# Down products with 64 slots and 512 weight columns at a time, and output rows moved 64 at a time, in a hybrid decoder block with 32 experts

## The chip, the cores and the metric

One Trainium2 chip, one core. The time is the device time of one launch in microseconds (us); the runs before the change took 1283.56 to 1284.55 us, with a median of 1284.49 us over 3 runs.

## The reference

A decoder block of 512 tokens and 1024 features: a gated linear recurrence and a dilated attention share one input and one output projection; a mixture of experts follows. The change touches only the latter. Cut to it (`h` are 512 normed rows, each token goes to 4 of 32 experts):

```python
logits = (h @ router_w + router_b).astype(jnp.float32)
top_vals, top_idx = lax.top_k(logits, TOP_K)
gates = jax.nn.softmax(top_vals, axis=-1)
...
def expert_block(args):
    xb, e = args
    u = xb @ w_up[e] + b_up[e]
    return _clamped_swiglu(u) @ w_down[e] + b_down[e]
...
y = ybuf[dest] * gates.reshape(-1)[order][:, None].astype(ybuf.dtype)
return jnp.zeros((N, D), h.dtype).at[sorted_tok].add(y)
```

All is float32. `w_up` is 1024 x 2048 and `w_down` 1024 x 1024 per expert, 12 MB together, so 384 MB of weights are read once. A final RMS norm over each row ends the block.

## The kernel before, in words

The kernel is written engine by engine: each engine has its own function with a fixed order of instructions and waits on semaphores. The first 300 us are projections, recurrence, attention and routing. Then come 32 steps, one per expert, in an order of experts by their load.

**Slots.** An expert takes its tokens in groups of 32 slots (`STEP`). Experts at place 0, 1 and the odd places to 29 have `BIG` = 3 groups (96 slots), the 16 others `LESS` = 2 (64 slots); `groups(p)` says which. Tokens beyond that go through further blocks at the end (`nx`), of which this input has none in its profile.

**TensorE's step** (`moe_step`, line 2174) for place p: bias rows of the up product (`up_bias`, L2072), 8 chunks of the up product (`up_chunk`, L2081), and, behind chunks 2 and 5, one turn each of the *move* of the outputs of expert p-2 (`move_turn`, L2153). Then the down product of expert p-1 (`down_chunk`, L2098), 4 chunks of two halves.

In up and down products the slots are the stationary operand, 32 columns wide, and the weights stream. Four such products stand beside each other in the array, one for each quarter of the output columns: `quarter(j)` chooses 32 output partitions. So the 32 rows of a group lie in four quarters of the partitions, each with 256 of the 1024 output features:

```python
ins = pe.matmul(Yp2[quarter(j), g, :], As[:, g, 2 * c + h, :], raw[q.slot(m)][:, at_w:at_w + 256],
```

**Outputs.** ACT scales the down product by the gates and writes its high part (fp32r) to SBUF (`y_highs`, L898), DVE the rest as low part (`y_lows`, L1571), per group. DVE makes for each group a 0/1 matrix that says which token a slot holds (`token_sels`, L1578). The move multiplies that matrix (stationary, 32 rows x 128 tokens) with high and low part, adding up in PSUM over groups and parts for each of 4 token tiles (`i`); DVE then adds PSUM to the rows `X` (`add_tile`, L1584). Before a down product TensorE waits for the low parts of the expert before (`y_low`) and, with 96 slots, for the adds.

**Weights.** SP loads pairs of chunks (2 MB) into 9 buffers; each load waits until TensorE has used the buffer (`chunk_used`), L562.

**Tail.** The last two experts' outputs go half by half of the features: `pair_chunk` (L2117), `last_chunk` (L2129), `move_half` (L2140). `move_half` takes two phases, with a wait between them, since two row groups may not write one bank at the same time. ACT's and DVE's `add_half` (L1591), squares, root and scaling end the program.

## Time and profile before

| | us |
|---|---|
| median of 3 runs (lowest, highest) | 1284.49 (1283.56, 1284.55) |
| the profiled execution, its own time | 1284.0 |
| its span, first to last instruction | 1282.2 |
| TensorE busy | 1245.9 (97%) |
| VectorE busy | 554.7 (43%) |
| ScalarE busy | 238.6 (19%) |
| GpSimd busy | 122.7 (10%) |

The profile is of one execution. The expert steps begin at about 300 us and end at 1266 us. In the rows, PE is TensorE's matmuls, PEld its weight loads, DVE VectorE, ACT ScalarE, POOL GpSimd, SP the engine that issues the DMAs. A matmul of fp32 stands in the trace as two records (192 for the 96 matmuls of a down product with 96 slots). Starts of matmuls are recorded; their ends are modelled. The granted TensorE clock is 1.00 of full speed in all stretches used below.

### The profile page before, as it was taken

How to read it: one execution, taken by the hardware profiler on the slowest of the kernel's cores; microseconds unless marked ns; L12 is line 12 of the kernel's file. 1: busy time of each engine (PE TensorE's matmuls, PEld its weight loads, DVE VectorE, ACT ScalarE, POOL GpSimd, SP SyncE). 2: the span in 40 equal slices, each digit the busy share in tenths (PEclk: the TensorE clock that was granted, in tenths of full speed). 3: DMA queues.
4: the chain of work that ended last, by engine and by line, in shares of the span. 5: the costliest groups of instructions: out<-in, count | busy, mean ns of one | idle time of the engine just before them, and what ended most of it. 6: DMA issues, size and time to landing. Idle time of an engine off the chain costs nothing.

```text
span 1282.2 us, 33934 instructions
## 1 busy us (share of the span) xinstructions
PE 1245.9 (97%) x15007; PEld 680.1 (53%) x15008; DVE 554.7 (43%) x1066; ACT 238.6 (19%) x463; POOL 122.7 (10%) x127
## 2 busy tenths in 40 slices
PE   6999999999999999999999999999999999999994
PEld 5888887884455544444444444444444454444442
DVE  5657648665544533333333424233323333332423
ACT  6354436421100001000000001000100000000104
POOL 0000005200110110101010101010110101010001
PEclk9999999999999999999999999999999999999998
DMA  8422208069899999999999999999999999999983
GB/s 241 134 66 82 84 1 331 21 264 423 346 412 380 416 426 419 425 424 423 423 423 424 423 425 423 424 422 425 421 423 423 423 424 424 423 423 424 424 353 144
DMA packets 69547, 444.26 MB, mean 346 GB/s; under 512 B 6537, under 2 KB 35821, under 8 KB 44721
## 3 DMA queue, kind: packets, MB, share of 16 engines
q1 hardware_dynamic: 65696, 433.61, 82.6%
q0 software_dynamic: 3696, 8.38, 1.8%
q8 instruction: 123, 2.02, 0.6%
q14 instruction: 32, 0.25, 0.1%
HBM read 439.10 MB, written 4.72 MB: 346 GB/s over the span
## 4 chain that ended last, share of the span: by engine, by line
PE 92%; DMA 4%; DVE 2%; ACT 1%; issue 1%; SPq 0%; DVEq 0%
PE psum L2081 43%; PE psum L2098 20%; PE psum L1807 9%; PE psum L2153 6%; PE psum L1804 3%; DMA w_raw_pair<-w_down 3%; PE psum L2072 2%; PE psum L1892 2%; PE psum L1950 1%; PE psum L1925 1%; PE psum L2129 1%; PE psum L1967 1%; DMA shape_consts<-shape_constants 1%; PE psum L1769 1%; PE psum L1905 1%
## 5 line engine op out<-in xcount | busy, mean ns | idle before, releaser
L2081 PE MATMUL psum<-w_raw_pair,x_slots_turned 128*32 128x512 f32 x4928 | 551.0, 594 | 2.0 <-DVE x_slots_turned L1649 0.7
L2081 PEld LDWEIGHTS psum<-w_raw_pair,x_slots_turned 128*32 128x32 f32 x4928 | 168.5, 110 | 317.7 <-issue 296.9
L1584 DVE TENSOR_TENSOR x_rows<-x_rows,psum 128x1024 f32<-128x1024 f32 x120 | 141.1, 1217 | 330.7 <-PE psum L2153 330.7
L2098 PE MATMUL psum<-w_raw_pair,a_slots 128*32 128x256 f32 x4864 | 272.3, 379 | 1.2 <-DMA w_raw_pair<-w_down 1.1
L2098 PEld LDWEIGHTS psum<-w_raw_pair,a_slots 128*32 128x32 f32 x4864 | 164.9, 110 | 116.0 <-issue 21.8
L889 ACT ACTIVATE lin<-psum 128x768 f32<-128x768 f32 (+1 forms) x32 | 22.5, 704 | 606.3 <-PE psum L2081 606.3
L1553 DVE STREAM_TRANSPOSE a_slots<-glu 128x768 f32<-128x768 f32 (+1 forms) x31 | 26.3, 849 | 183.4 <-PE psum L2098 183.4
L2153 PEld LDWEIGHTS psum<-y_part_group,token_sel 32*128 32x128 f32 x2432 | 76.7, 184 | 48.7 <-issue 48.6
L686 POOL COPY gather_quarters<-row_quarters 128x2 int32 (+1 forms) x30 | 16.5, 550 | 761.1 <-DVE x_slots_turned L1548 704.3
L2153 PE MATMUL psum<-y_part_group,token_sel 32*128 32x256 f32 x2432 | 88.8, 287 | 0.0
L898 ACT ACTIVATE y_part_group<-psum,gate_t 128x256 fp32r<-128x256 f32 x76 | 31.0, 471 | 255.6 <-PE psum L2098 245.0
L691 POOL DMA_INDIRECT gathered_quarters<-normed_rows,gather_quarters x74 | 74.7, 1010 | 39.3 <-POOL gather_quarters L686 24.7
L1807 PE MATMUL psum<-h_low,w_in_high 128*128 128x512 f32 x160 | 63.3, 396 | 0.0
L1807 PE MATMUL psum<-h_high,w_in_high 128*128 128x512 f32 x160 | 62.3, 389 | 0.0
L1807 PE MATMUL psum<-h_high,w_in_low 128*128 128x512 f32 x160 | 62.3, 389 | 0.0
L1548 DVE STREAM_TRANSPOSE x_slots_turned<-gathered_quarters 128x256 f32<-128x256 f32 x74 | 43.5, 631 | 42.2 <-PE psum L2081 40.4
L1571 DVE SCALAR_TENSOR_TENSOR y_part_group<-psum,gate_t,y_part_group 128x256 fp32r<-128x256 f32 x76 | 32.6, 478 | 22.9 <-ACT y_part_group L898 22.9
L1070 DVE TENSOR_TENSOR w_in_low<-w_in_raw,w_in_high 128x1024 fp32r<-128x1024 f32 x24 | 29.0, 1221 | 17.2 <-ACT w_in_high L768 17.2
L1807 PEld LDWEIGHTS psum<-h_low,w_in_high 128*128 128x128 f32 x160 | 30.1, 188 | 6.9 <-issue 0.6
L1807 PEld LDWEIGHTS psum<-h_high,w_in_low 128*128 128x128 f32 x160 | 30.0, 188 | 6.4
L1807 PEld LDWEIGHTS psum<-h_high,w_in_high 128*128 128x128 f32 x160 | 30.1, 188 | 5.8
L1578 DVE TENSOR_SCALAR token_sel<-token_numbers,slot_tokens 128x512 fp32r<-128x512 f32 x76 | 32.6, 480 | 0.0
(312 smaller groups left out, 990.8 us busy)
## 6 DMA issues: line engine op xcount, KB each, us to landing
w_raw_pair<-w_up SPq DMA_DIRECT2D x128, 2048.0 KB, 26.5
w_raw_pair<-w_down SPq DMA_DIRECT2D x60, 2048.0 KB, 25.5
w_in_raw<-w_in SPq DMA_DIRECT2D x28, 512.0 KB, 3.8
w_raw_pair<-w_down SPq DMA_DIRECT2D x8, 1024.0 KB, 36.6
w_buf<-w_out SPq DMA_DIRECT2D x4, 1024.0 KB, 11.1
x_rows<-x SPq DMA_DIRECT2D x4, 512.0 KB, 5.3
x_rows<-x SPq DMA_DIRECT2D x1, 2048.0 KB, 13.2
normed_rows<-h_rows SPq DMA_DIRECT2D x4, 512.0 KB, 4.5
```

The lines of the kernel that those rows point to most:

```text
L691: pool.indirect_dma_start(XQ[:, g, :], None, normed_dram.rearrange("r (j f) -> (r j) f", j=4), bass.IndirectOffsetOnAxis(IDXQ[:, g:g + 1], 0),
L898: ins = act.activation(YP[0][g][:, :], banks[:, g, :], ACT.Copy, scale=gate_t[:, g, bass.ds(column, 1)])
L1070: ins = dve.tensor_tensor(WPL[:, c % 4, :, :], WPR[:, c % 2, :, :], WPH[:, c % 4, :, :].bitcast(F32), ALU.subtract)
L1548: ins = dve.transpose(xq[:, g, :, :], XQ[:, g, :].rearrange("p (i k) -> p k i", k=DK))
L1571: ins = dve.scalar_tensor_tensor(YP[1][g][:, :], banks[:, g, :], gate_t[:, g, bass.ds(column, 1)], YP[0][g][:, :].bitcast(F32), ALU.mult, ...
L1578: ins = dve.tensor_scalar(sels[g][:, :], tokens[:, :], slot_tok[:, g, bass.ds(column, 1)], None, ALU.is_equal)
L1584: dve.tensor_tensor(x_tile, x_tile, PS[:, first_bank:first_bank + 4, half], ALU.add).then_inc(added, 1)
L1804: ins = pe.matmul(blocks_of(o), h_part[:, k, j * P:(j + 1) * P], w_rows, start=(k == 0 and h_part is HL), stop=(k == DK - 1 and w_part is ...
L1807: ins = pe.matmul(o, w_part[:, j, k, :], h_part[:, k, :], start=(k == 0 and h_part is HL), stop=(k == DK - 1 and w_part is WPL))
L2081: ins = pe.matmul(U[quarter(j), g, :], slots, up_columns(w, j), start=False, stop=(c == UPC - 1))
L2098: ins = pe.matmul(Yp2[quarter(j), g, :], As[:, g, 2 * c + h, :], raw[q.slot(m)][:, at_w:at_w + 256], start=(c + h == 0 and g % 2 == 0), st ...
L2153: ins = pe.matmul(PS[:, MOVE_BANK + j, i % 2 * 256:i % 2 * 256 + 256], SELT[g][quarter(j), i * P:(i + 1) * P], YP[part][g][quarter(j), :], ...
```

## The change

The three groups no longer stand alike. The first two become one *wide* group of 64 slots, the third stays as it is.

- Down product: the wide group is a stationary operand of 64 columns, two pieces beside each other (`side(j)`: 64 partitions), each against 512 weight columns. With 96 slots the third group follows in the same half chunk, 4 pieces of 32 columns against 256.
- `a_slots` is laid out so that 64 or 96 slots are adjacent; DVE's transpose writes it with another stride.
- ACT and DVE write high and low part of the wide group with one instruction of 512 columns (`Y_wide`), and of the third with one of 256. Token matrices are 2 for 96 slots, 1 for 64.
- Moves: the wide group is moved in pieces of 64 rows. With 64 slots, 2 matmuls of 512 columns per tile and part. With 96 slots, 4 of 256 columns, then the third group's 4 of 32 rows, for each tile and each part.
- Tail: the same with 256 columns; the phases and their waits fall away, and DVE may add the first two tiles when `half_moved` is signalled. The copies to `slot_pair` and `gate_pair` go.

```diff
--- before.py
+++ after.py
+PAIR = LESS * STEP
+WIDE, THIRD = range(2)
+GROUP_IN = ((0, 1, 0, 1), (2, 2, 2, 2))
...
-        As = over("a_slots", [P, BIG, 2 * DNC, STEP], xg0 + 13312)
-        As_last = over("a_slots_last", [P, LESS, 2 * DNC, STEP], xg0 + 4096)
+        As = over("a_slots", [P, 2 * DNC, BLK], xg0 + 13312)
+        As_last = over("a_slots_last", [P, 2 * DNC, PAIR], xg0 + 4096)
...
-        y_piece_at = [[oa0, oa0 + 1024, oa0 + 4096], [oa0 + 2048, oa0 + 3072, oa0 + 5120]]
-        YP = [[over(f"y_part{part}_group{g}", [P, 256], y_piece_at[part][g], F32R) for g in range(BIG)] for part in range(2)]
-        YP_last = [[YP[part][2], over(f"y_last_part{part}", [P, 256], xg0 + 2048 + part * 1024, F32R)] for part in range(2)]
+        YW = [over(f"y_wide_part{part}", [P, HALF], oa0 + part * 2048, F32R) for part in range(2)]
+        YT = [over(f"y_third_part{part}", [P, 256], oa0 + 4096 + part * 1024, F32R) for part in range(2)]
+        YP = [[over(f"y_part{part}_half{n}", [P, 256], oa0 + part * 2048 + n * 1024, F32R) for n in range(2)] for part in range(2)]
+        YP_last = [[YT[part], over(f"y_last_part{part}", [P, 256], xg0 + 2048 + part * 1024, F32R)] for part in range(2)]
...
+        Y_wide, Y_third = PS[:, 3, :], Yp2[:, LESS, :]
...
+        def side(j):
+            return slice(j * PAIR, (j + 1) * PAIR)
...
-            def y_highs(n, column, banks):
-
-                for g in range(n):
-                    ins = act.activation(YP[0][g][:, :], banks[:, g, :], ACT.Copy, scale=gate_t[:, g, bass.ds(column, 1)])
-                    if g:
-                        ins.then_inc(y_high, 1)
+            def y_highs(n, column):
+
+                act.activation(YW[0][:, :], Y_wide, ACT.Copy, scale=gate_t[:, WIDE, bass.ds(column, 1)]).then_inc(y_high, 1)
+                if n == BIG:
+                    act.activation(YT[0][:, :], Y_third, ACT.Copy, scale=gate_t[:, THIRD, bass.ds(column, 1)]).then_inc(y_high, 1)
...
             def a_rows(q, n, slots):
                 dve.wait_ge(a_ready, q + 1)
-                dve.transpose(slots[:, 0:n, :, :].rearrange("p g b s -> p (g b s)"), GL[:, 0:n, :].rearrange("p g f -> p (g f)")
-                              ).then_inc(a_turned, 1)
+                dve.transpose(slots[:, :, 0:n * STEP].rearrange("p b (g s) -> p g b s", s=STEP),
+                              GL[:, 0:n, :].rearrange("p g (b f) -> p g b f", f=STEP)).then_inc(a_turned, 1)
...
-            def y_lows(highs, n, column, banks):
-
-                for g in range(n):
-                    if g != 1:
-                        dve.wait_ge(y_high, highs + max(g, 1))
-                    ins = dve.scalar_tensor_tensor(YP[1][g][:, :], banks[:, g, :], gate_t[:, g, bass.ds(column, 1)],
-                                                   YP[0][g][:, :].bitcast(F32), ALU.mult, ALU.subtract)
+            def y_lows(highs, n, column):
+
+                dve.wait_ge(y_high, highs + 1)
+                ins = dve.scalar_tensor_tensor(YW[1][:, :], Y_wide, gate_t[:, WIDE, bass.ds(column, 1)], YW[0][:, :].bitcast(F32),
+                                               ALU.mult, ALU.subtract)
+                if n == BIG:
+                    dve.wait_ge(y_high, highs + 2)
+                    ins = dve.scalar_tensor_tensor(YT[1][:, :], Y_third, gate_t[:, THIRD, bass.ds(column, 1)], YT[0][:, :].bitcast(F32),
+                                                   ALU.mult, ALU.subtract)
                 ins.then_inc(y_low, 1)
 
-            def token_sels(n, column, sels):
-
-                for g in range(n):
-                    ins = dve.tensor_scalar(sels[g][:, :], tokens[:, :], slot_tok[:, g, bass.ds(column, 1)], None, ALU.is_equal)
+            def token_sels(n, column):
+
+                ins = dve.tensor_scalar(SELT[0][:, :], tokens[:, :], slot_tok[:, WIDE, bass.ds(column, 1)], None, ALU.is_equal)
+                if n == BIG:
+                    ins = dve.tensor_scalar(SELT[1][:, :], tokens[:, :], slot_tok[:, THIRD, bass.ds(column, 1)], None, ALU.is_equal)
                 ins.then_inc(token_sel, 1)
...
+            def add_tile(i, n):
+
+                if n == BIG:
+                    x_tile = X[:, i, :].rearrange("p (j f) -> p j f", j=4)
+                    sums = PS[:, MOVE_BANK:MOVE_BANK + 4, i % 2 * 256:i % 2 * 256 + 256]
+                else:
+                    x_tile = X[:, i, :].rearrange("p (j f) -> p j f", j=2)
+                    sums = PS[:, MOVE_BANK + 2 * (i % 2):MOVE_BANK + 2 * (i % 2) + 2, :]
+                dve.tensor_tensor(x_tile, x_tile, sums, ALU.add).then_inc(added, 1)
...
             def add_half(n, i):
 
+                if i < 2:
+                    dve.wait_ge(S("half_moved"), n + 1)
+                else:
+                    dve.wait_ge(moved, NE * 2 - 2 + 2 * n)
...
-            def pair_columns():
-
-                for g in range(2):
-                    r = slice(2 * g * STEP, 2 * (g + 1) * STEP)
-                    dve.tensor_copy(slot_pair[r, :], slot_tok[r, g, 0:NE])
-                    ins = dve.tensor_copy(gate_pair[r, :], gate_t[r, g, 0:NE])
-                ins.then_inc(S("pair_columns"), 1)
...
             def down_chunk(q, m, c, n):
                 if c % 2 == 0:
                     pe.wait_ge(raw_landed[q.slot(m) // 2], q.landed(m))
+                w = raw[q.slot(m)]
                 for h in range(2):
-                    for g in range(n):
+                    first, last = c + h == 0, c == DNC - 1 and h == 1
+                    for j in range(2):
+                        at_w = h * D + j * HALF
+                        ins = pe.matmul(Y_wide[side(j), :], As[:, 2 * c + h, 0:PAIR], w[:, at_w:at_w + HALF], start=first, stop=last)
+                    if n == BIG:
                         for j in range(4):
                             at_w = h * D + j * 256
-                            ins = pe.matmul(Yp2[quarter(j), g, :], As[:, g, 2 * c + h, :], raw[q.slot(m)][:, at_w:at_w + 256],
-                                            start=(c + h == 0 and g % 2 == 0), stop=(c == DNC - 1 and h == 1),
-                                            skip_group_check=True)
+                            ins = pe.matmul(Y_third[quarter(j), :], As[:, 2 * c + h, PAIR:BLK], w[:, at_w:at_w + 256],
+                                            start=first, stop=last)
                 ins.then_inc(chunk_used, 1)
...
+            def move_half(n, tiles, sel, parts, first):
+
+                for i in tiles:
+                    for part in range(2):
                         for j in range(2):
+                            ins = pe.matmul(PS[:, HALF_BANKS[n][i // 2][j], i % 2 * 256:i % 2 * 256 + 256], sel[side(j), i * P:(i + 1) * P],
+                                            parts[part][side(j), :], start=(first and i % 2 + part == 0), stop=(not first and part == 1),
+                                            skip_group_check=True)
+                    if not first and i == 1:
+                        ins.then_inc(S("half_moved"), 1)
...
             def move_turn(turn, n, first):
 
                 pe.sem_inc(S("moves_begun"), 1)
                 for i in (2 * turn, 2 * turn + 1):
-                    for g in range(n):
-                        for part in range(2):
+                    tile, cols = slice(i * P, (i + 1) * P), slice(i % 2 * 256, i % 2 * 256 + 256)
+                    for part in range(2):
+                        if n == BIG:
+                            for w in range(2):
+                                for j in range(2):
+                                    pe.matmul(PS[:, MOVE_BANK + 2 * j + w, cols], SELT[0][side(j), tile], YW[part][side(j), w * 256:w * 256 + 256],
+                                              start=(first and i % 2 + part == 0), stop=False, skip_group_check=True)
                             for j in range(4):
-                                ins = pe.matmul(PS[:, MOVE_BANK + j, i % 2 * 256:i % 2 * 256 + 256], SELT[g][quarter(j), i * P:(i + 1) * P],
-                                                YP[part][g][quarter(j), :], start=(first and i % 2 + g + part == 0),
-                                                stop=(g == n - 1 and part == 1), skip_group_check=True)
+                                ins = pe.matmul(PS[:, MOVE_BANK + j, cols], SELT[1][quarter(j), tile], YT[part][quarter(j), :],
+                                                start=False, stop=(part == 1), skip_group_check=True)
+                        else:
+                            for j in range(2):
+                                ins = pe.matmul(PS[:, MOVE_BANK + 2 * (i % 2) + j, :], SELT[0][side(j), tile], YW[part][side(j), :],
+                                                start=(part == 0), stop=(part == 1))
                 ins.then_inc(moved, 1)
...
-            move_half(0, 0, SELT[0], (YP[0][0], YP[1][0]), True).then_inc(S("crossed"), 1)
+            move_half(0, (0, 1), SELT[0], (YP[0][0], YP[1][0]), True)
             last_chunk(0, 1)
-            pe.wait_ge(S("crossed"), 1)
-            move_half(0, 1, SELT[0], (YP[0][0], YP[1][0]), True).then_inc(moved, 1)
+            move_half(0, (2, 3), SELT[0], (YP[0][0], YP[1][0]), True).then_inc(moved, 1)
             last_chunk(1, 0)
             pe.wait_ge(token_sel, NE)
             pe.wait_ge(S("first_low"), 1)
-            pe.wait_ge(moved, NE * 2 - 3)
-            move_half(0, 0, SELT_last, (YP_last[0][0], YP_last[1][0]), False).then_inc(S("crossed"), 1)
-            pe.wait_ge(S("crossed"), 2)
-            move_half(0, 1, SELT_last, (YP_last[0][0], YP_last[1][0]), False).then_inc(moved, 1)
+            move_half(0, range(TT), SELT_last, (YP_last[0][0], YP_last[1][0]), False).then_inc(moved, 1)
             last_chunk(1, 1)
             pe.wait_ge(added, ADDS - 2 * TT + 2)
-            move_half(1, 0, SELT[0], (YP[0][1], YP[1][1]), True).then_inc(S("crossed"), 1)
-            pe.wait_ge(S("crossed"), 3)
-            move_half(1, 1, SELT[0], (YP[0][1], YP[1][1]), True).then_inc(moved, 1)
+            move_half(1, range(TT), SELT[0], (YP[0][1], YP[1][1]), True).then_inc(moved, 1)
             pe.wait_ge(y_low, NE)
-            pe.wait_ge(moved, NE * 2 - 1)
-            move_half(1, 0, SELT_last, (YP_last[0][1], YP_last[1][1]), False).then_inc(S("crossed"), 1)
-            pe.wait_ge(S("crossed"), 4)
-            move_half(1, 1, SELT_last, (YP_last[0][1], YP_last[1][1]), False).then_inc(moved, 1)
+            move_half(1, range(TT), SELT_last, (YP_last[0][1], YP_last[1][1]), False).then_inc(moved, 1)
```

On TensorE, the down product of a 96-slot expert, with the end of the up product before it and the bias and up product behind it. Columns: line, operation, output and inputs, size of the output, count. `w_raw_pair_123` and `_115` hold two chunks each; before:

```order
L2081 MATMUL psum<-w_raw_pair_122,x_slots_turned 32x512 x16
L2098 MATMUL psum<-w_raw_pair_123,a_slots 32x256 x48
L2098 MATMUL psum<-w_raw_pair_115,a_slots 32x256 x48
L2072 MATMUL psum<-bias_up_parts,bias_sel_up 32x512 x12
L2081 MATMUL psum<-w_raw_pair_116,x_slots_turned 32x512 x24
```

The same place with the change:

```order
L2094 MATMUL psum<-w_raw_pair_122,x_slots_turned 32x512 x16
L2112 MATMUL psum<-w_raw_pair_123,a_slots 64x512 x2
L2116 MATMUL psum<-w_raw_pair_123,a_slots 32x256 x4
...
L2112 MATMUL psum<-w_raw_pair_115,a_slots 64x512 x2
L2116 MATMUL psum<-w_raw_pair_115,a_slots 32x256 x4
...
L2085 MATMUL psum<-bias_up_parts,bias_sel_up 32x512 x12
L2094 MATMUL psum<-w_raw_pair_116,x_slots_turned 32x512 x24
```

The 96 matmuls of one size became 16 of 64 columns and 32 of 32 columns, which alternate 8 times.

On TensorE, one turn of a move of 96 slots, between two chunks of the up product (`y_part_group` and `token_sel` are the parts and token matrices of a group); before:

```order
L2081 MATMUL psum<-w_raw_pair_117,x_slots_turned 32x512 x12
L2153 MATMUL psum<-y_part_group_134,token_sel_161 128x256 x4
L2153 MATMUL psum<-y_part_group_137,token_sel_161 128x256 x4
L2153 MATMUL psum<-y_part_group_135,token_sel_162 128x256 x4
L2153 MATMUL psum<-y_part_group_138,token_sel_162 128x256 x4
L2153 MATMUL psum<-y_part_group_136,token_sel_163 128x256 x4
L2153 MATMUL psum<-y_part_group_139,token_sel_163 128x256 x4
...
L2081 MATMUL psum<-w_raw_pair_117,x_slots_turned 32x512 x12
```

With the change:

```order
L2094 MATMUL psum<-w_raw_pair_117,x_slots_turned 32x512 x12
L2169 MATMUL psum<-y_wide_part_134,token_sel_161 128x256 x4
L2172 MATMUL psum<-y_third_part_136,token_sel_162 128x256 x4
L2169 MATMUL psum<-y_wide_part_135,token_sel_161 128x256 x4
L2172 MATMUL psum<-y_third_part_137,token_sel_162 128x256 x4
...
L2094 MATMUL psum<-w_raw_pair_117,x_slots_turned 32x512 x12
```

The rows stand for one of the two tiles of a turn. 12 groups of four matmuls with 32 rows became 8: in turn four matmuls with 64 rows (L2169) and four with 32 (L2172).

## Rows read from the trace of the kernel before

**Rows 1.** Busy time of each engine in a stretch, with granted clock and DMA.

```profile
core 0: us, PE busy (x) PEld busy (x) DVE busy (x) ACT busy (x) POOL busy (x), PEclk, DMA share, GB/s
500.00:1200.00 700.00, 697.58 (x9646) 315.40 (x9642) 239.36 (x339) 59.16 (x129) 73.28 (x83) 1.00 1.01 423
```

**Rows 2.** DMA issues (us to landing) from 340 to 400, then from 1100 to 1200.

```profile
w_raw_pair<-w_up SPq DMA_DIRECT2D x8, 2048.0 KB, 10.7
...
w_raw_pair<-w_up SPq DMA_DIRECT2D x14, 2048.0 KB, 37.6
```

**Rows 3.** Timeline of PE: start, us, instructions; two steps from 737 us.

```profile
737.03 10.54 PE L2098 MATMUL psum<-w_raw_pair,a_slots 128*32 128x256 f32 x192
...
755.88 1.70 PE L2153 MATMUL psum<-y_part_group,token_sel 32*128 32x256 f32 x48
757.51 7.93 PE L2081 MATMUL psum<-w_raw_pair,x_slots_turned 128*32 128x512 f32 x72
765.37 1.70 PE L2153 MATMUL psum<-y_part_group,token_sel 32*128 32x256 f32 x48
...
772.18 7.27 PE L2098 MATMUL psum<-w_raw_pair,a_slots 128*32 128x256 f32 x128
779.09 1.09 PE L2072 MATMUL psum<-bias_up_parts,bias_sel_up 96*32 96x512 bf16 x8
...
785.62 1.22 PE L2153 MATMUL psum<-y_part_group,token_sel 32*128 32x256 f32 x32
786.77 5.36 PE L2081 MATMUL psum<-w_raw_pair,x_slots_turned 128*32 128x512 f32 x48
...
796.67 3.64 PE L2098 MATMUL psum<-w_raw_pair,a_slots 128*32 128x256 f32 x64
```

**Rows 4.** Timeline of PE, then of DVE, from 1215 us to the tail.

```profile
1215.19 10.57 PE L2098 MATMUL psum<-w_raw_pair,a_slots 128*32 128x256 f32 x192 [1.10 <-DMA w_raw_pair<-w_down]
...
1252.80 1.93 PE L2129 MATMUL psum<-w_raw_pair,a_slots_last 128*32 128x256 f32 x32 [0.74 <-DMA w_raw_pair<-w_down]
1254.66 0.74 PE L2140 MATMUL psum<-y_part_group,token_sel 32*128 32x256 f32 x16
1255.34 1.93 PE L2129 MATMUL psum<-w_raw_pair,a_slots_last 128*32 128x256 f32 x32
1257.20 0.74 PE L2140 MATMUL psum<-y_part_group,token_sel 32*128 32x256 f32 x16
...
1259.92 1.56 PE L2140 MATMUL psum<-y_part_group,token_sel_last 32*128 32x256 f32 x32
1261.41 1.93 PE L2129 MATMUL psum<-w_raw_pair,a_slots_last 128*32 128x256 f32 x32
...
1264.33 1.27 DVE L1591 TENSOR_TENSOR x_rows<-x_rows,psum 128x512 f32<-128x512 f32 x2
1266.61 2.48 DVE L1591 TENSOR_TENSOR x_rows<-x_rows,psum 128x512 f32<-128x512 f32 x4 [1.01 <-PE psum L2140]
```

**Rows 5.** Timeline of PE and PEld where one product follows another.

```profile
174.08 1.12 PE L1820 MATMUL psum<-ak_T,aq_T 64*128 64x512 f32 x4
175.13 0.19 PEld L1804 LDWEIGHTS psum<-w_in_high,h_low 128*128 128x128 f32 x1 [0.76 <-issue]
...
289.08 0.41 PEld L1967 LDWEIGHTS psum<-router_w_sb,h_T 128*128 128x128 f32 x3 [0.41 <-issue]
...
747.17 0.55 PEld L2072 LDWEIGHTS psum<-bias_up_parts,bias_sel_up 96*32 96x32 bf16 x12
...
754.48 1.47 PE L2081 MATMUL psum<-w_raw_pair,x_slots_turned 128*32 128x512 f32 x12
755.88 0.19 PEld L2153 LDWEIGHTS psum<-y_part_group,token_sel 32*128 32x128 f32 x4 [0.84 <-issue]
```

**Rows 6.** Groups of instructions by line: busy, mean ns, idle before and releaser.

```profile
L1553 DVE STREAM_TRANSPOSE a_slots<-glu 128x768 f32<-128x768 f32 x16 | 15.6, 978 | 76.6 <-PE psum L2098 76.6
L898 ACT ACTIVATE y_part_group<-psum,gate_t 128x256 fp32r<-128x256 f32 x76 | 31.0, 471 | 255.6 <-PE psum L2098 245.0
```

97 lines of the change are left out of this document (41 added, 56 removed).

## The prediction

> **What bounds the kernel now.** I read the page first: TensorE is busy for 97% of the span, which proves little with pipelined matmuls. Then the stages. From 500 to 1200 us TensorE hardly stops (697.6 of 700 us), and the DMA engines are full too, at 423 GB/s [rows 1]. Which of the two sets the pace is told by the time from the issue of a weight load to its landing: 10.7 us around 370 us, 37.6 us around 1150 us [rows 2]. A load is issued when TensorE frees its buffer, so the queue grows all the time: TensorE frees buffers slightly faster than the DMAs fill them, and lives on what was loaded ahead. Its period for two experts is 796.67 - 737.03 = 59.6 us [rows 3]; the DMAs' must be a little longer. The stock lasts until about 1214 us. Only then does TensorE wait for weights, three times for long: idle for 1.10 us before 1215.19 and 0.74 before 1252.80 are the first and last [rows 4]. The ends of matmuls are modelled and lie late, 1.93 us for 8 rounds that take 1.73 (below), so some 0.2 us comes to each: 1.3, 1.3 and 0.9, together 3.5 us. So both paths end almost together. TensorE time taken out of the loop brings next to nothing, since the DMAs stay full; TensorE time put into it is paid in full beyond those 3.5 us. DVE (239 of 700 us) and ACT (59) have ample room [rows 1].
>
> **How TensorE spends a step.** The trace records each fp32 matmul as two. Four of 32 columns run side by side: 72 records of the up product are 18 rounds of four and last 7.93 us, 48 are 12 rounds and last 5.36 [rows 3]. The difference makes 0.428 us a round. From start to start the 18 rounds take 765.37 - 757.51 = 7.86 us [rows 3], 0.15 us more than their rounds, once per visit. The down product with 64 slots is 32 rounds with 256 columns in 779.09 - 772.18 = 6.91 us, 0.216 a round [rows 3], so 48 rounds with 96 slots are 10.4. A last down chunk, 8 rounds, takes 1257.20 - 1255.34 = 1.86 us [rows 4], 0.13 more than its rounds. The moves, weights of 128 columns and 32 rows: 12 rounds in 757.51 - 755.88 = 1.63 us, 8 in 786.77 - 785.62 = 1.15, 4 in 1255.34 - 1254.66 = 0.68 [rows 3, 4]. That is 0.119 us a round and 0.20 us per visit.
>
> What is this price per visit? Between down product, bias and up product, all with 32 weight columns, it does not occur: the bias's weight loads start at 747.17, while the down product's last round still streams [rows 5] (48 rounds from 737.03 end at 747.4). At a move it does. The last up round of 12 records starts at 754.48 + 2 x 0.43 = 755.34 and streams to 755.77; the move's loads start at 755.88, after 0.84 us of idle loader, against 0.30 between rounds [rows 5]. Nothing is loaded ahead: the array empties first (0.11 us), then the load itself is bare. The same is seen where only the columns change, from 32 to 128 (0.41 us idle before 289.08, behind L2001), and where only the rows do, from 64 to 128 (0.76 us before 175.13) [rows 5]. **So each change of the shape of the piece of the array in use costs 0.13 to 0.20 us**, the more the more columns are then loaded. No row has a change between 64 and 32 columns, or 64 and 32 rows. The Trainium skill, TensorEngine Tiling (Array Packing), Key Properties and Available Configurations, speaks against this change there: changing the tiling mode, as opposed to the tile, drains the engine, and 128x64 and 128x32, like 64x128 and 32x128, are listed as modes of their own.
>
> **The change, part by part.** Experts 0 and the odd ones to 29 hold 96 slots (16 experts); 14 others of the loop hold 64.
>
> *Down product, 64 slots.* 32 rounds of four (6.91 us) become 16 rounds of two with 512 columns. A round streams twice as long as before, like the up product's: 16 x 0.428 = 6.85 us. New are the entry with 64 columns and the way back to 32 for the bias. For 64 columns I take 0.16 us a visit, between 0.14 (32 columns) and 0.20 (128 columns), nearer the former. In all 6.85 + 0.16 + 0.14 - 6.91 = +0.24 us. The skill's page TensorE: Matmul & The Clock Gate, LDWEIGHTS, counts a load as columns divided by 1.2 ns, 53 ns for 64 columns against 27 for 32; by that, an estimate, the visit would be 0.17 us and the sum less than 1 us higher. No row has a load of 64 columns.
>
> *Down product, 96 slots.* Here each of the 8 halves of chunks now goes from 64 columns to 32 and back. Wide part: 0.16 + 2 x 0.428 = 1.02 us. Third: 0.14 + 2 x 0.216 = 0.57 us. 8 x 1.59 = 12.7 us instead of 10.4: **+2.3 us**. The bias behind it has 32 columns again and costs no further visit.
>
> *Moves, 64 slots.* A turn of 8 rounds at 256 columns (1.15 us) becomes 4 rounds of two with 512 columns, in one mode: 0.20 + 4 x 0.216 = 1.06; two turns, -0.18 us.
>
> *Moves, 96 slots.* A turn of 12 rounds in one visit (1.63 us) becomes four times a wide part (2 rounds, 0.20 + 0.24 = 0.44) and a third (1 round, 0.20 + 0.12 = 0.32): 4 x 0.76 = 3.03 us. **+1.40 us** a turn, +2.80 per expert.
>
> *ACT and DVE.* Of three evictions per expert at 471 ns on ACT, and their like on DVE, two become one of 512 columns: between 471 and 2 x 471 ns, so no more work in all [rows 6]. One token selection goes per expert. The transpose moves the same elements with another write stride; its price for that is not in the trace, but between nothing and twice its 978 ns it stays hidden, as DVE works a third of the time [rows 1, 6]. All of it lies beside TensorE: the low parts must be ready at the first move, 755.88 - 747.4 = 8.5 us behind the down product [rows 3], and the waits before the adds stand where they stood. If that cover were gone it would be at most 1 us an expert. Counted 0. The four pair-column copies go too, 0 as well. SP issues the same loads in the same order.
>
> *Tail.* The first two pieces keep their 4 rounds. A half moved for all four tiles was two phases with a wait between, 1261.41 - 1259.92 = 1.49 us, and is now 0.20 + 8 x 0.119 = 1.15: -0.34 us for the one ahead of the last chunk. Behind the last chunk DVE finished the first half at 1264.33 + 1.27 = 1265.60 and waited until 1266.61 [rows 4]; moves now end sooner and the first two tiles are signalled early, so it goes on at once: -1.0 us. DVE's adds are late next. Together -1.4 us.
>
> **Sum.** 16 x (2.3 + 2.8) = 81.6; 14 x (0.24 - 0.18) = 0.8; waits for weights gone, -3.5, since TensorE's period of 59.6 + 5.2 = 64.8 us is now well above what the DMAs need; tail -1.4. That is +77.5 us on the profiled execution's 1284.0: **1361.5, rounded 1362**. The median of the runs, 1284.49, is 0.5 higher, which I leave in the rounding. Bounds: 128 wide visits at 0.14 or 0.20 instead of 0.16 give -2.6 or +5.1 us. For 96 slots there are 16 x 16 = 256 visits more in the down products and 16 x 2 x 7 = 224 more in the moves; if a visit of a single round hides a third of its price, some 25 us go.
>
> **Rivals.**
>
> 1. *The array does not empty between 64 and 32.* The hardware could treat the pieces as the same small squares and load ahead, as between bias and up product. For: those two differ in rows (96 and 128) at no price [rows 5]. Against: every other change of shape in the trace pays. The rounds' streaming is the same with wide and narrow pieces, so the loop is where it was and only the tail's 1.4 us come: 1282.6, not slower. It decides when a further visit costs under 0.016 us: 480 of them then stay within the 3.5 us of waits, the tail's 1.4 and the 2.6 us that a measurement can tell. Chance 9%, a third of it faster by over 0.2%.
>
> 2. *Only changes of rows cost, columns are free.* Then the down products add nothing and the moves 16 x 2.8 = 45: 1284.0 + 45 - 3.5 - 1.4 = 1324. 5%.
>
> 3. *Two pieces of 64 columns do not run side by side.* Then every down product streams 6.85 us longer: 30 x 6.85 = 206 more, about 1567. Against: 64-row pieces do run in pairs, four records of 512 columns from 174.08 to the next load at 175.13, where one by one they would need 4 x 0.43 = 1.7 us [rows 5]. 2%.
>
> 4. *The copies are what counts:* wider evictions or the transpose hold up the next move. This would show as TensorE waiting for DVE; 8.5 us of room speak against it, at most 1 us an expert, 32 more: 1394. 2%.
>
> **How the numbers follow.** The forecast, each change of shape paid as measured, has 82%. The range 1322 to 1380 takes in rival 2, the part hidden in short visits, and upwards the 5 us for wide loads and some 13 us for visits dearer than the long ones; outside lie rivals 1, 3 and 4 and the forecast's edges, about 2 in 10. A measurement of this kernel tells 0.2% (2.6 us) from no change. Faster 3% and same 7%, rival 1 with a remainder for what I don't see; slower 90%.
>
> **What would show it.** Right: in the order of time the down product of a 96-slot expert takes 12.7 us instead of 10.4 and a move turn 3.0 instead of 1.6, with gaps before each switch between the wide and the third lines; two experts take 64.8 us; loads land about 10 us or less after their issue to the end, and no wait for weights is left. The down product of a 64-slot expert stays near 7.0 us. Wrong: if weights of the third part are loaded while the wide part streams (rival 1), if only the moves grow (2), or if the 64-slot down product takes near 14 us (3).

## The result and the profile after

The changed kernel takes **1347.87 us** (median of 4 runs, 1347.31 to 1348.94) against 1284.52 (4 runs, 1283.56 to 1285.37): a ratio of 1.0496, 95% interval 1.0484 to 1.0509, 63.4 us slower. The forecast was +77.5 us, so its sign and most of its size came, and about 14 us did not. The profiled executions, 1347.94 and 1284.0 us, differ by 63.9; the ledger below is made for these two.

Two experts, from the timeline of PE of the changed kernel (start, us, instructions), in the order of [rows 3]:

```profile
765.83 1.08 PE L2112 MATMUL psum<-w_raw_pair,a_slots 128*64 128x512 f32 x4
766.84 0.64 PE L2116 MATMUL psum<-w_raw_pair,a_slots 128*32 128x256 f32 x8
767.41 1.08 PE L2112 MATMUL psum<-w_raw_pair,a_slots 128*64 128x512 f32 x4
...
778.34 0.83 PE L2085 MATMUL psum<-bias_up_parts,bias_sel_up 96*32 96x512 bf16 x12
...
786.83 0.51 PE L2169 MATMUL psum<-y_wide_part,token_sel 64*128 64x256 f32 x4
787.27 0.39 PE L2172 MATMUL psum<-y_third_part,token_sel 32*128 32x256 f32 x4
...
789.85 7.93 PE L2094 MATMUL psum<-w_raw_pair,x_slots_turned 128*32 128x512 f32 x72
...
800.72 5.36 PE L2094 MATMUL psum<-w_raw_pair,x_slots_turned 128*32 128x512 f32 x48
806.01 7.09 PE L2112 MATMUL psum<-w_raw_pair,a_slots 128*64 128x512 f32 x32
813.03 0.61 PE L2085 MATMUL psum<-bias_up_parts,bias_sel_up 96*32 96x512 bf16 x8
813.47 5.33 PE L2094 MATMUL psum<-w_raw_pair,x_slots_turned 128*32 128x512 f32 x48
818.73 1.20 PE L2176 MATMUL psum<-y_wide_part,token_sel 64*128 64x512 f32 x8
819.85 5.36 PE L2094 MATMUL psum<-w_raw_pair,x_slots_turned 128*32 128x512 f32 x48
...
829.84 1.08 PE L2112 MATMUL psum<-w_raw_pair,a_slots 128*64 128x512 f32 x4
```

Read it from start to start. The period is 829.84 - 765.83 = 64.0 us (before 59.6, forecast 64.8). The down product of the 96-slot expert takes 778.34 - 765.83 = 12.51 us: a wide visit 1.01, a third 0.57, eight times. A move turn of a 96-slot expert takes 789.85 - 786.83 = 3.02 us, and the down product of a 64-slot expert 7.02 ("near 7.0" in the forecast). These three are within 0.2 us of the forecast; the period is 0.8 us short of it, because the 59.6 us of before held 0.8 us that was not work, as the runs below show.

The same timeline with the loader (PEld), at the first switch:

```profile
765.83 0.20 PEld L2112 LDWEIGHTS psum<-w_raw_pair,a_slots 128*64 128x64 f32 x4 [0.84 <-issue]
...
766.84 0.16 PEld L2116 LDWEIGHTS psum<-w_raw_pair,a_slots 128*32 128x32 f32 x8 [0.81 <-issue]
```

The loader stands idle for 0.81 us of the wide visit, although what it loads next has long been in SBUF: here the 32-column piece is loaded only when the wide part has streamed. The run without a change of width, below, tests whether the width is the reason. Under rival 1 this pause would have been absent.

In the stage from 500 to 1200 us (first row, columns as in [rows 1]) TensorE has no pause that the profile shows, and the DMAs now have some slack. The second row, from the DMA issues between 1100 and 1200 us, ends with the time from issue to landing of the loads of `w_up`: 12.4 us, where it was 37.6 in [rows 2]. The six loads of `w_down` took 9.3 us. The forecast said about 10 or less.

```profile
500.00:1200.00 700.00, 700.00 (x5996) 225.60 (x5992) 214.03 (x275) 52.13 (x99) 68.33 (x77) 1.00 0.98 403
```

```profile
w_raw_pair<-w_up SPq DMA_DIRECT2D x12, 2048.0 KB, 12.4
```

No wait for weights of the experts is left. The tail answers to [rows 4]. First the start of its first product in the kernel before, then PE and DVE of the changed kernel:

```profile
1243.67 5.36 PE L2117 MATMUL psum<-w_raw_pair,a_slots 128*32 128x256 f32 x96
```

```profile
1310.98 7.13 PE L2133 MATMUL psum<-w_raw_pair,a_slots 128*64 128x256 f32 x64
...
1325.29 1.21 PE L2153 MATMUL psum<-y_third_part,token_sel_last 64*128 64x256 f32 x16
1326.43 1.95 PE L2144 MATMUL psum<-w_raw_pair,a_slots_last 128*64 128x256 f32 x16
```

```profile
1329.34 3.67 DVE L1614 TENSOR_TENSOR x_rows<-x_rows,psum 128x512 f32<-128x512 f32 x6
```

A half for all four tiles is moved in 1326.43 - 1325.29 = 1.14 us (1.49 before), and DVE adds six times without a pause, where it had stood for 1.01 us.

### The profile page after: what moved, and what is told of

It reads as the page before. It is cut to its first block, busy times and chain, and to the rows that moved or that the text cites. A ratio compares the mean times of both kernels' runs of the same rounds, so it can differ in the third digit from the quotient of the medians.

```text
span 1346.1 us, 25227 instructions
## 1 busy us (share of the span) xinstructions
PE 1315.6 (98%) x10751; PEld 577.3 (43%) x10752; DVE 536.3 (40%) x994; ACT 231.2 (17%) x431; POOL 123.0 (9%) x127
## 3 DMA queue, kind: packets, MB, share of 16 engines
q8 instruction: 91, 1.49, 0.5%
## 4 chain that ended last, share of the span: by engine, by line
PE 95%; DVE 2%; ACT 1%; issue 0%; DMA 0%; SPq 0%; DVEq 0%; ACTq 0%
PE psum L2094 41%; PE psum L2112 17%; PE psum L1820 8%; PE psum L2116 5%; PE psum L2169 4%; PE psum L1817 3%; PE psum L2172 3%; PE psum L2176 2%; PE psum L1905 1%; PE psum L2085 1%; PE psum L1963 1%; PE psum L1938 1%; PE psum L1980 1%; PE psum L2144 1%; PE psum L2133 1%; PE psum L1918 1%
## 5 line engine op out<-in xcount | busy, mean ns | idle before, releaser
L2094 PEld LDWEIGHTS psum<-w_raw_pair,x_slots_turned 128*32 128x32 f32 x4928 | 151.7, 110 | 335.5 <-issue 324.2
L2112 PE MATMUL psum<-w_raw_pair,a_slots 128*64 128x512 f32 x960 | 237.3, 607 | 0.0
L2112 PEld LDWEIGHTS psum<-w_raw_pair,a_slots 128*64 128x64 f32 x960 | 56.2, 135 | 127.2 <-issue 127.2
L2116 PE MATMUL psum<-w_raw_pair,a_slots 128*32 128x256 f32 x1024 | 81.8, 391 | 0.0
L903 ACT ACTIVATE y_wide_part<-psum,gate_t 128x512 fp32r<-128x512 f32 x30 | 20.6, 687 | 274.7 <-PE psum L2116 179.8
L2116 PEld LDWEIGHTS psum<-w_raw_pair,a_slots 128*32 128x32 f32 x1024 | 20.1, 108 | 103.9 <-issue 103.9
L2169 PE MATMUL psum<-y_wide_part,token_sel 64*128 64x256 f32 x512 | 64.4, 330 | 0.0
L2169 PEld LDWEIGHTS psum<-y_wide_part,token_sel 64*128 64x128 f32 x512 | 38.1, 184 | 38.2 <-issue 25.8
L2172 PE MATMUL psum<-y_third_part,token_sel 32*128 32x256 f32 x512 | 50.0, 379 | 0.0
L2176 PE MATMUL psum<-y_wide_part,token_sel 64*128 64x512 f32 x224 | 33.5, 417 | 0.0
```

The costliest lines, as they stand in the source:

```text
L2094: ins = pe.matmul(U[quarter(j), g, :], slots, up_columns(w, j), start=False, stop=(c == UPC - 1))
L2112: ins = pe.matmul(Y_wide[side(j), :], As[:, 2 * c + h, 0:PAIR], w[:, at_w:at_w + HALF], start=first, stop=last)
L2116: ins = pe.matmul(Y_third[quarter(j), :], As[:, 2 * c + h, PAIR:BLK], w[:, at_w:at_w + 256], start=first, stop=last)
L2169: pe.matmul(PS[:, MOVE_BANK + 2 * j + w, cols], SELT[0][side(j), tile], YW[part][side(j), w * 256:w * 256 + 256], start=(first and i % 2 + ...
L2172: ins = pe.matmul(PS[:, MOVE_BANK + j, cols], SELT[1][quarter(j), tile], YT[part][quarter(j), :], start=False, stop=(part == 1), skip_grou ...
L2176: ins = pe.matmul(PS[:, MOVE_BANK + 2 * (i % 2) + j, :], SELT[0][side(j), tile], YW[part][side(j), :], start=(part == 0), stop=(part == 1))
```

## The experiments

Weights, instructions and data stay as in the changed kernel unless a text says otherwise. The visits come first, then the 14 us that the forecast had too much.

### One move turn, two visits instead of eight

```diff
-                for i in (2 * turn, 2 * turn + 1):
+                for wide in ((True, False) if n == BIG else (True,)):
+                    for i in (2 * turn, 2 * turn + 1):
...
-                        if n == BIG:
+                            if n == BIG and wide:
...
+                            elif n == BIG:
```

> The changed kernel, with the output move of a 96-slot expert written in another order: in each turn first the 64-slot parts of both tiles and both parts, then the thirds, so that TensorE changes its array piece 2 times a turn and not 8. The same instructions otherwise. Theory (the price is paid at each change of piece, 0.20 us for a visit of the 64-column piece and one of the 32-column piece together with the exposed load): a turn of 3.02 us has 8 visits of about 0.17 us, 6 of them go, so a turn takes about 1.9 to 2.0 us; 2 turns times 16 experts, so 34 to 38 us less, 1310 to 1314 us. Rival (the thirds and the 64-slot parts are slow for another reason, the instructions of the two column halves or writes to the same bank, whatever their order): a turn stays at 3.0 us and the time at 1348 us.

Measured: 1310.74 us (4 runs, 1310.17 to 1312.09; ratio to the kernel before 1.0208, 1.0193 to 1.0224), 37.1 us under the changed kernel. Its timeline of PE has one turn as

```profile
770.74 1.22 PE L2170 MATMUL psum<-y_wide_part,token_sel 64*128 64x256 f32 x16
771.88 0.74 PE L2174 MATMUL psum<-y_third_part,token_sel 32*128 32x256 f32 x16
772.55 0.64 PE L2094 MATMUL psum<-w_raw_pair,x_slots_turned 128*32 128x512 f32 x4
```

772.55 - 770.74 = 1.81 us for the same 32 records that took 3.02. Six visits fewer save 1.2 us: 0.20 each, the price of the prediction. The expectation had 0.17 a visit, and so a turn of 1.9 to 2.0 us: a turn gained slightly more than that. The rival (3.0 us whatever the order) falls.

### The down product in four visits instead of sixteen

```diff
+            def down_pair(q, m, c):
...
+                for wide in (True, False):
+                    for k in range(2):
+                        w = raw[q.slot(m + k)]
+                        for h in range(2):
...
+                            for j in range(2 if wide else 4):
```

> The changed kernel, with the down product of a 96-slot expert written in another order: for each pair of weight chunks first the 64-slot products of its four halves, then the thirds, so that there are 4 visits of pieces an expert and not 16. The same instructions otherwise. Theory (each visit costs 0.14 to 0.16 us over its streaming): 12 visits less, 1.7 to 1.9 us of the 12.5 us that the down product takes, 16 experts: 27 to 31 us less, 1317 to 1321 us. Rival (only the second sort of products is slow, or the two sorts hide each other's loads as they stand): 12.5 us stay, 1348 us.

Measured: 1320.53 us (4 runs, 1320.10 to 1321.01; ratio 1.0283, 1.0267 to 1.0299), 27.3 us less. From its timeline of PE:

```profile
754.07 3.65 PE L2132 MATMUL psum<-w_raw_pair,a_slots 128*64 128x512 f32 x16
757.65 1.93 PE L2135 MATMUL psum<-w_raw_pair,a_slots 128*32 128x256 f32 x32
759.52 3.65 PE L2132 MATMUL psum<-w_raw_pair,a_slots 128*64 128x512 f32 x16
763.10 1.93 PE L2135 MATMUL psum<-w_raw_pair,a_slots 128*32 128x256 f32 x32
764.85 0.40 PE L2085 MATMUL psum<-bias_up_parts,bias_sel_up 96*32 96x512 bf16 x4
```

10.78 us instead of 12.51: 1.73 / 12 = 0.144 us a visit.

### Both orders

> The changed kernel with both orders at once: per 96-slot expert 12 visits less in the down product and 12 less in the moves. Theory: the two gains add, 61 to 69 us, which gives 1279 to 1287 us; an expert pair would take about 60 us, and by then the weights' loads are as late as in the kernel before, so the waits for them come back and the end is bounded near 1281 to 1285 us. Rival (the gains are not of the array but of what lies beside it): less than the sum, 1300 us or more.

Measured: 1282.38 us (11 runs, 1281.64 to 1284.26; ratio 0.9987, 0.9978 to 0.9996). Both savings add: 1347.9 - 37.1 - 27.3 = 1283.5. One term of the expectation was wrong in kind. DMA stands at 424 GB/s again in the window from 500 to 1200 us, but TensorE's 700.00 us of that window show no wait for weights:

```profile
500.00:1200.00 700.00, 700.00 (x6426) 246.06 (x6426) 224.47 (x289) 55.01 (x104) 73.45 (x83) 1.00 1.01 424
```

So 12 + 12 visits less per 96-slot expert are worth the whole loss in time: **order alone turns 5% slower into no slower**. The visits that stay still cost: a down product of 10.78 + 0.11 us against 10.36 and a turn of 1.81 against 1.63 make some 14 us over 16 experts. They are offset by about as much lost time that the kernel before has and this one has not, which is the subject of the last sections.

### No change of width, the same alternation

```diff
-                            ins = pe.matmul(Y_third[quarter(j), :], As[:, 2 * c + h, PAIR:BLK], w[:, at_w:at_w + 256],
-                                            start=first, stop=last)
+                            ins = pe.matmul(Y_third[side(j % 2), :], As[:, 2 * c + h, STEP:BLK], w[:, at_w:at_w + 256],
+                                            start=first, stop=last, skip_group_check=True)
```

> The changed kernel, where the third group's down products of a 96-slot expert hold 64 slots too (the last 64 of the 96) in 64-column pieces, four matmuls of 256 weight columns for a half of a chunk; both column halves are added in one place, so the third group's products are not those of the reference. The two sorts of products alternate as before, but no piece changes width. Theory (the change of the piece's width drains the array): a half of a chunk is 0.86 us for the first group and 0.86 us for the third, the down product takes about 13.8 us and no load stands bare after a product; 16 experts, about 1368 us. Rival (it is the alternating of groups, stationary data or target that costs, whatever the width): the pauses stay, about 2.0 us a half and 16.3 us a product, about 1408 us.

Measured: 1372.95 us (one run; the kernel before had a median of 1282.26 on that chip). From its timelines of PE and PEld:

```profile
777.23 1.08 PE L2112 MATMUL psum<-w_raw_pair,a_slots 128*64 128x512 f32 x4
778.14 1.03 PE L2116 MATMUL psum<-w_raw_pair,a_slots 128*64 128x256 f32 x8
779.01 1.03 PE L2112 MATMUL psum<-w_raw_pair,a_slots 128*64 128x512 f32 x4
779.87 0.39 PE L2116 MATMUL psum<-w_raw_pair,a_slots 128*64 128x256 f32 x2
```

```profile
777.72 0.14 PEld L2116 LDWEIGHTS psum<-w_raw_pair,a_slots 128*64 128x64 f32 x2 [0.28 <-issue]
```

Here the third's weights are loaded at 777.72, while the wide part still streams until about 778.1 (0.28 us of idle loader, not 0.81). After the first visit a half of a chunk takes 0.87 + 0.86 us, all streaming, and the whole product 13.9 (its bias starts at 791.16). The theory had 1368 us, the rival 1408. So in the down product groups, targets and data alternate at no price that these rows show; it is the piece's width that costs. For the moves the kernel before is the like case: its turn alternates three groups and two parts, all with 32 rows, in one visit of 1.63 us.

### The new layout without the mixed experts

```diff
-                    for j in range(2):
+                    for j in range(2 if n == LESS else 0):
...
-                    if n == BIG:
+                    for g in range(BIG if n == BIG else 0):
...
-                            ins = pe.matmul(Y_third[quarter(j), :], As[:, 2 * c + h, PAIR:BLK], w[:, at_w:at_w + 256],
+                            ins = pe.matmul(Yp2[quarter(j), g, :], As[:, 2 * c + h, quarter(g)], w[:, at_w:at_w + 256],
```

> The changed layout for 64-slot experts and the tail only; 96-slot experts as in the kernel before (three groups of 32 slots, no 64-column piece). Theory: the loss sits entirely in the 96-slot experts, so it goes: 1280 to 1284 us, against 1284.5 before; the bias block of a 64-slot step takes 0.44 us and not 1.21 to 1.25 us, the tail is about 1.2 us shorter, and the rest of the gain is taken by waits for weights, since loads bound the kernel then. Rival (the 64-slot experts have a cost of their own in the new layout, which the 96-slot ones hide): above 1286 us.

Measured: 1278.48 us (5 runs, 1278.07 to 1280.64; ratio **0.9959**, 0.9945 to 0.9972): faster than both kernels, by 5.8 us (0.4%) against the one before. Timeline of PE at a 64-slot step, then its two largest waits for weights (us in total, times, longest; with two smaller ones 7.7 us). The profile is of the slowest of the five, 1280.64 us:

```profile
767.27 7.09 PE L2121 MATMUL psum<-w_raw_pair,a_slots 128*64 128x512 f32 x32
774.29 0.61 PE L2094 MATMUL psum<-bias_up_parts,bias_sel_up 96*32 96x512 bf16 x8
774.73 0.60 PE L2103 MATMUL psum<-w_raw_pair,x_slots_turned 128*32 128x512 f32 x4
```

```profile
PE psum L2125 <- DMA w_raw_pair<-w_down: 4.4, 4, 1.3
PE psum L2142 <- DMA w_raw_pair<-w_down: 1.7, 2, 1.1
```

The bias block behind the 64-slot down product takes 0.44 us. In the kernel before it takes 779.09 to 780.30 = **1.21 us** [rows 3 has its start]; here is the row behind it:

```profile
780.30 1.96 PE L2081 MATMUL psum<-w_raw_pair,x_slots_turned 128*32 128x512 f32 x16
```

Two rounds of 0.216 us need 0.44. Nothing that the profile names is waited for. At two places the loader's next load starts only 0.66 and 0.69 us after the one before it (idle for 0.57 and 0.60 us in its timeline), among instructions that wait for nothing late: the pair of weights that comes next landed 15 us earlier, and the semaphores that stand before the bias and the first up round were raised 5 us earlier. This is the term that the forecast did not have. The next runs ask what it is.

### The 64-slot down product in as many instructions as before

In the changed kernel, then in the kernel just above, a half of a chunk takes 8 matmuls of 128 weight columns and not 2 of 512 (the edit in the changed kernel):

```diff
+                    for k in range(1 if n == BIG else 4):
+                        cols = HALF if n == BIG else P
...
-                        at_w = h * D + j * HALF
+                            at_w = h * D + j * HALF + k * cols
+                            ins = pe.matmul(Y_wide[side(j), k * cols:(k + 1) * cols], As[:, 2 * c + h, 0:PAIR], w[:, at_w:at_w + cols],
+                                            start=(first and k == 0), stop=last, skip_group_check=True)
```

> The changed kernel, with the down product of a 64-slot expert cut into pieces of 128 weight columns: the same columns stream through the same pieces of the array, but by four times as many matmuls and loads. Theory (the 1.21 to 1.25 us of the bias block ahead of each 64-slot step in the kernel before is TensorE waiting for its next instructions, after a product of many short ones): the bias block of a 64-slot step goes from 0.44 us back to about 1.2 us or more, the product itself takes 7.0 us or little more; 14 steps, so 10 us or more on top: 1358 us or more. Rival (that time in the kernel before has to do with the 32-column pieces): 0.44 us stay and the time is 1348 us.

Measured: 1349.94 us (4 runs, 1349.41 to 1350.57; ratio 1.0527, 1.0507 to 1.0548), and 0.44 us for each of the bias blocks: by the words of the expectation the rival. One of them, behind a down product that started at 807.21 (7.14 us):

```profile
814.35 0.61 PE L2085 MATMUL psum<-bias_up_parts,bias_sel_up 96*32 96x512 bf16 x8
814.79 0.60 PE L2094 MATMUL psum<-w_raw_pair,x_slots_turned 128*32 128x512 f32 x4
```

But the run was on a chip where the kernel before takes 1282.26 us (7 runs, 1279.50 to 1284.52) and not 1284.3, which matters below.

> The kernel with the changed layout for 64-slot experts and the tail only, with the down product of a 64-slot expert cut into pieces of 128 weight columns: as many matmuls and loads as in the kernel before at the same place, with the moves of the 96-slot experts ahead of them as dense as there, but in 64-column pieces. Theory (TensorE takes its instructions faster than they are supplied through dense moves followed by a dense down product, and runs dry at the bias block behind them): the bias block of a 64-slot step takes 1.2 us again and not 0.44 us; the waits for weights shrink by part of it, so 1279 to 1284 us. Rival (the 0.8 us belong to the 32-column pieces of the 64-slot down product): 0.44 us stay and the time is that of the kernel without the cut, 1278 to 1279 us.

Measured: 1284.34 us (11 runs, 1282.24 to 1286.16; ratio 0.9998, 0.9989 to 1.0007), 5.9 us more than without the cut. This is yet another chip; the kernel before takes 1284.24 on it, and 1284.26 on that of the run without the cut. Timeline of PE:

```profile
774.38 7.20 PE L2122 MATMUL psum<-w_raw_pair,a_slots 128*64 128x128 f32 x126
781.76 0.38 PE L2122 MATMUL psum<-w_raw_pair,a_slots 128*64 128x128 f32 x2 [0.17 <-issue]
782.07 1.04 PE L2094 MATMUL psum<-bias_up_parts,bias_sel_up 96*32 96x512 bf16 x8
782.75 1.65 PE L2103 MATMUL psum<-w_raw_pair,x_slots_turned 128*32 128x512 f32 x12
```

The pause is back, with 64-column pieces: 782.07 - 774.38 = 7.69 us for the product (7.14 in the run just above), 0.68 for the bias. So it does not need 32-column pieces. Between these two kernels the time lost goes with the number of TensorE's instructions at this place, the columns being equal. But they ran on different chips, and the run just above has the same dense down product without the pause. No run has this kernel cut and uncut on one chip, so the number of instructions is likely a part of the cause and not shown to be it.

### Fewer instructions in the moves ahead of it

In the kernel before:

```diff
-                        for part in range(2):
+                        for part in range(1 if n == BIG else 2):
...
-                                                stop=(g == n - 1 and part == 1), skip_group_check=True)
+                                                stop=(g == n - 1 and part == (0 if n == BIG else 1)), skip_group_check=True)
```

> The kernel before, with the low parts of the 96-slot experts' outputs left out of their moves: half of the matmuls and loads of these moves go (24 of 48 in a turn), so its output lacks that correction. The 64-slot down products keep their 32-column pieces and all their instructions. Theory (supply of instructions): the store that TensorE has ahead is larger when the down product begins, so the bias block of a 64-slot step takes 0.44 us, or clearly less than 1.2 us; rival (32-column pieces): 1.2 us stay. The moves themselves lose 0.8 us a turn, 26 us in all, but the loads of the weights bound the kernel then, so the time should be 1275 to 1281 us either way.

Measured: 1279.03 us (one run; 1284.24 before). The time came as expected, with 14 us of waits for weights. But the bias blocks take 1.36 to 1.39 us (the first 1.52), not less than 1.21:

```profile
826.56 0.39 PE L2072 MATMUL psum<-bias_up_parts,bias_sel_up 96*32 96x512 bf16 x2
...
827.94 1.53 PE L2081 MATMUL psum<-w_raw_pair,x_slots_turned 128*32 128x512 f32 x12
```

The unchanged kernel, profiled on yet another chip below, has 1.34 to 1.39 us in most steps. So half of the moves' instructions made no difference that shows. My picture of a store that dense moves use up is wrong, or too simple.

### Half of the weight traffic

In the kernel before, then in the one with the new layout for 64 slots and the tail, for experts 10 and later (`part` is 2 there):

```diff
-                sp.dma_start(pair_raw[q.slot(m) // 2][:, :], src).then_inc(raw_landed[q.slot(m) // 2], 16)
+                sp.dma_start(pair_raw[q.slot(m) // 2][:, 0:2 * D * 2 // part], src[:, 0:2 * D * 2 // part]).then_inc(raw_landed[q.slot(m) // 2], 16)
```

> The kernel before, with each weight load of experts 10 and later cut to its first half of columns; the other half of a buffer keeps an older expert's weights, so these experts' outputs are not the reference's. All matmuls, loads of TensorE and waits stay. Theory (the 0.8 us that TensorE loses at the bias block of a 64-slot step come from the number of its instructions alone): the block takes 1.2 us still. Rival (TensorE's instructions come late because their transfers share the DMA engines with weights at 424 GB/s): the block takes 0.44 us once the loads are halved, from about 560 us on. The waits for weights, 3.5 us in all, go either way: 1280 to 1283 us by the theory, 1271 to 1275 by the rival.

> The kernel with the changed layout for 64-slot experts and the tail only, with the weight loads halved in the same way. It tells what this kernel still loses to its weights: the trace shows some 8 us of waits for weights in it. Theory (by then the loads are the bound, and TensorE's own work is less): 1269 to 1273 us. Rival (the waits only cover what TensorE would lose anyway): 1277 us or more.

Measured on one chip, one run each: 1266.99 and 1267.19 us; the unchanged kernel takes 1281.07 there. Both are below every range of their expectations. From expert 1's step on no bias block is longer than its rounds in either (0.44 us, 0.65 with 12 records), not even before expert 10, where the loads are whole. So halving is not what removed the pause, and I ran the unchanged kernel and the first of the two again, side by side.

> The kernel before, unchanged, profiled once more, on the same chip as the next run. In the run with half loads the bias block of the 64-slot steps took 0.44 us from the first step on, also ahead of the first halved load, so it may be a matter of the chip or of the execution. If it is of the kernel alone, the block takes 1.2 us again in most 64-slot steps; if of the execution, it may take 0.44 us in all of them, and the time is then 1281 us or less.

> The kernel before with the loads of experts 10 and later halved, once more, beside the unchanged kernel on the same chip. If the late instructions of TensorE come from sharing the DMA engines with the weights, the blocks up to about 540 us are as long as in the unchanged kernel's profile, and 0.44 us behind it; if from the number of instructions alone, they are as long as there throughout; if neither run shows any block over 0.44 us, the cause lies in the execution and stays open.

Measured, both on one more chip: 1285.0 us unchanged, 1283.63 with half the loads. Windows of 500 us (columns as above), first the unchanged kernel on this chip, then half the loads on this chip, then half the loads on the chip of the pair before:

```profile
600.00:1100.00 500.00, 497.19 (x6816) 240.72 (x6812) 173.34 (x244) 42.25 (x93) 51.10 (x58) 1.00 1.01 423
```

```profile
600.00:1100.00 500.00, 497.77 (x6824) 238.68 (x6822) 174.81 (x247) 42.48 (x93) 50.48 (x58) 1.00 0.67 223
```

```profile
600.00:1100.00 500.00, 500.00 (x6984) 221.45 (x6977) 175.22 (x248) 42.85 (x94) 52.04 (x59) 1.00 0.68 230
```

The same program, with the same traffic of 223 to 230 GB/s, gets 6824 matmuls done on one chip and 6984 on the other in 500 us. A 64-slot step on the two, PE's timeline, with the pause and without:

```profile
899.48 0.48 PE L2072 MATMUL psum<-bias_up_parts,bias_sel_up 96*32 96x512 bf16 x3
899.59 0.38 PE L2098 MATMUL psum<-w_raw_pair,a_slots 128*32 128x256 f32 x1
900.10 0.60 PE L2072 MATMUL psum<-bias_up_parts,bias_sel_up 96*32 96x512 bf16 x5
900.85 2.73 PE L2081 MATMUL psum<-w_raw_pair,x_slots_turned 128*32 128x512 f32 x21
```

```profile
890.04 0.62 PE L2072 MATMUL psum<-bias_up_parts,bias_sel_up 96*32 96x512 bf16 x8
890.47 1.04 PE L2081 MATMUL psum<-w_raw_pair,x_slots_turned 128*32 128x512 f32 x8
```

The pause is there with half the traffic (1.37 us) and absent with all of it (0.44 us in the four steps with 64 slots before the first halved load, on the other chip): sharing the DMA engines with weights is not its cause. It is a matter of the chip or the execution, and most likely of the program too: none of the kernels with 12799 or fewer matmuls shows it in its 64-slot steps, and four of them were profiled on the chip where the kernel before takes 1284.26 us, about its time where the pause is seen. A profile of the kernel before on that very chip is missing. That executions of one program differ on one chip is also seen without a profile: 1279.50 to 1284.52 us over seven runs, above.

Nor do the packets of instructions explain it. The trace has them on queue q8, 16 KB each, and from 400 to 1200 us of the profile before there are 86, one for every 257 records of PE and PEld, so they must be mostly TensorE's. In the two steps shown one starts 2.12 us ahead of the bias block with the pause and 2.10 us ahead of the one without. Over the 64-slot steps of the kernel before, the last packet ahead of the block's end starts anywhere from 7.6 us before the block begins to 0.7 us after, and the pause is there all the same.

What stays open: what holds TensorE up in the one execution and not in the other, why fewer moves did not shorten it, and whether the 0.44 us of the run with 128 columns in the changed kernel came from its thinner program or from its chip.

These runs also tell how the kernel before is bounded. Where the pause is, half the loads bring 0.6 to 1.4 us (against two runs of the unchanged kernel): TensorE is the bound. On the chip without the pause they bring 14 us, so there the loads must be; the unchanged kernel has no profile on that chip to show its waits.

## Why the prediction was right, and where it was off

- **What bounds the kernel: right in kind.** TensorE time put in was paid nearly in full, and the waits for weights went. "TensorE time taken out brings next to nothing" was too strong: 5.8 us came in the kernel with the new layout for 64 slots alone. Part of TensorE's 59.6 us was not work. The loads landed 12.4 us after their issue late in the loop, and not "about 10 us or less".
- **Down product, 96 slots.** Forecast +2.3 us per expert; measured 12.51 + 0.11 (the array empties at the end of the up product ahead, 8 rounds of which take 3.57 us instead of 3.46) - 10.36 = +2.26.
- **Moves, 96 slots.** Forecast +1.40 a turn; measured 3.02 - 1.63 = +1.39. With the line above: 16 x (2.26 + 2.78) = 80.6 us, forecast 81.6. Not in the forecast: the first expert's two turns, where the down biases are moved with 32 rows right ahead of the wide part, pay one more visit each, 1.08 instead of 0.78 us, +0.6 in all.
- **64 slots.** The down product is 7.02 - 6.91 + 0.12 (12 up rounds ahead of it, 5.29 instead of 5.17 us) = +0.23, forecast +0.24. The moves take 1.13 us a turn, not 1.06: -0.04 and not -0.18. So +2.7 us over 14 experts, forecast +0.8.
- **The step that failed: "Down product, 64 slots", +0.24 us.** Its start-to-start times were right, but the sum stopped at the product's last matmul. Behind it, in the kernel before, the bias block lost 0.8 us in most 64-slot steps. The whole loss can be read against the profile of the same program at 1266.99 us, which has no such pause. Down product, bias and the up product behind them are longer in the profile before by 0.83 to 1.08 us at each of the 13 steps with 64 slots whose down product starts from 414 to 1130 us, and by 13.3 us over the run, without the waits for weights. In the profile after no bias block from 325 us on is longer than its rounds. These 13.3 us lay in the baseline and are gone in the changed kernel, with 10751 matmuls and not 15007; why they are gone is open, as said above. The row was among those that I read [rows 3]: 779.09 with 8 records, whose two rounds need 0.44 us. I used its start and never asked for its end.
- **Waits for weights -3.5 and tail -1.4.** Measured -3.5, and -1.2 beyond the waits inside the tail: 1282.2 - 1243.67 = 38.5 us from its first product to the end before, 1346.1 - 1310.98 = 35.1 after.
- **Start.** Code that the change does not touch is 1.1 us earlier in the profile after: the bias of expert 1's step starts at 325.18, not 326.30.

Sum: 80.6 + 0.6 + 2.7 - 13.3 - 3.5 - 1.2 - 1.1 = 64.8, measured 63.9.

- **Rivals.** 1 and 2 (no emptying between 64 and 32 columns) fall with the loader's 0.81 us and with both regrouped kernels; 3 with 7.02 us for the wide down product; 4 because TensorE waits for DVE or ACT nowhere in the loop of experts where it had not waited before.
- **The Trainium skill,** TensorEngine Tiling (Array Packing), Key Properties and Available Configurations: that a change of mode drains and a change of tile does not is what the trace and the run without a change of width show; the price, 0.14 to 0.20 us, is from the runs. The Trainium skill's page TensorE: Matmul & The Clock Gate, LDWEIGHTS, would make a wide visit in the down product 27 ns dearer than a third (an estimate from its rate). The trace shows 1.01 - 0.86 = 0.15 us against 0.57 - 0.43 = 0.14, a smaller difference, as far as the rows resolve it.

## What to carry to other kernels

Count the changes of the array piece's shape, not the matmuls. Fewer instructions with the same columns lost 5% here because 480 more visits at 0.14 to 0.20 us came in. Ordering the same instructions by shape brought the time back to that of before, and leaving the mixed experts in one shape was faster than either kernel.

Before a stage is called bound by an engine's work, compare each block of the trace with its rounds, also the small one of 8 records that lies between two large ones. Time that no named wait explains is part of the baseline, and it may be gone after a change that never aimed at it.
